# Freeing raw weight slabs by two counts, and rounding the next part's first block sums earlier, in a two-block transformer kernel

## The reference

```python
    x = layer_norm(ALPHA * x + mix, ln1_g, ln1_b)
    up = causal_dwconv(jnp.einsum('bsd,df->bsf', x, w_up), ffn_conv_w)
    a, b = jnp.split(up, 2, axis=-1)
    ffn = jnp.einsum('bsf,fd->bsd', jax.nn.silu(a) * b, w_down)
    return layer_norm(ALPHA * x + ffn, ln2_g, ln2_b)
```

## Time and profile before

| | |
|---|---|
| median of the runs | 2868.78 us |
| the profiled execution's own time | 2869.09 us |
| its span | 2867.3 us |
| PE busy | 2828.6 us, 15082 matmuls |
| ACT busy | 1717.4 us |
| DVE busy | 1488.8 us |
| POOL busy | 407.3 us |
| granted TensorE clock | 0.999 |
| HBM read | 482.23 MB, 169 GB/s over the span |

### The profile page before, as it was taken

One profiled execution on the slowest core, in us unless ns is written; L12 is line 12 of the kernel. 1 busy time (PEld: TensorE's weight loads), 2 busy tenths in 40 slices (PEclk: granted clock), 3 DMA queues, 4 the chain that ended last, 5 costly groups with the idle time before them and its releaser, 6 DMA issues.

```text
span 2867.3 us, 40191 instructions
## 1 busy us (share of the span) xinstructions
PE 2828.6 (99%) x15082; PEld 2422.0 (84%) x15082; DVE 1488.8 (52%) x2661; ACT 1717.4 (60%) x2505; POOL 407.3 (14%) x472
## 2 busy tenths in 40 slices
PE   9999999999999999999999999999999999999999
PEld 7989889889997778888987887898877788789887
DVE  6654636364444654644326115677654611656865
ACT  7676767566665765655556545656554744665564
POOL 1111111111111001111110111111111011111110
PEclk9999999999999999999999999999999999999999
DMA  9776767788887428888894797887879388778784
GB/s 246 159 155 139 176 135 160 159 191 193 190 191 164 88 53 190 196 195 191 193 192 101 169 195 164 193 189 170 198 165 200 82 188 194 168 184 183 181 195 118
DMA packets 137026, 486.82 MB, mean 170 GB/s; under 512 B 15344, under 2 KB 15600, under 8 KB 136720
## 3 DMA queue, kind: packets, MB, share of 16 engines
q0 software_dynamic: 67296, 233.01, 44.4%
q1 hardware_dynamic: 68688, 249.59, 30.9%
q10 hardware_dynamic: 864, 1.78, 0.2%
HBM read 482.23 MB, written 2.10 MB: 169 GB/s over the span
## 4 chain that ended last, share of the span: by engine, by line
PE 84%; DVE 7%; ACT 5%; DVEq 2%; issue 1%; DMA 0%; ACTq 0%
PE ps L1346 56%; PE ps L1515 10%; PE ps L1365 5%; PE ps L1774 3%; DVE arena L2716 1%; ACT arena_r L772 1%; DVE arena_r L2259 1%; PE ps L1465 1%; PE ps L1715 1%; PE ps L1694 1%; ACT wl L534 1%; ACT wh L527 1%; PE ps L1953 1%; ACT arena L1217 1%; DVEq L2248 1%
## 5 line engine op out<-in xcount | busy, mean ns | idle before, releaser
L527 ACT ACTIVATE wh<-raw 128x1024 fp32r<-128x1024 f32 (+2 forms) x465 | 468.4, 1007 | 671.1 <-PE ps L1346 579.5
L510 POOL DMA_DIRECT2D wl<-weights x465 | 405.4, 872 | 2424.6 <-ACT wl L534 2424.6
L1346 PE MATMUL ps<-HH,wh 128*128 128x512 f32 x1456 | 571.5, 393 | 2.9 <-DVE HL L2637 2.1
L1346 PE MATMUL ps<-HH,wl 128*128 128x512 f32 x1456 | 567.0, 389 | 0.0
L1346 PE MATMUL ps<-HL,wh 128*128 128x512 f32 x1456 | 566.8, 389 | 0.0
L534 ACT ACTIVATE wl<-raw 128x1024 fp32r<-128x1024 f32 (+2 forms) x465 | 463.8, 997 | 88.9 <-DVE arena L2255 88.9
L1346 PE MATMUL ps<-MH,wh 128*128 128x512 f32 x928 | 362.4, 391 | 1.0 <-DVE ML L2520 0.7
L1346 PE MATMUL ps<-MH,wl 128*128 128x512 f32 x928 | 361.2, 389 | 0.0
L1346 PE MATMUL ps<-ML,wh 128*128 128x512 f32 x928 | 361.1, 389 | 0.0
L1346 PEld LDWEIGHTS ps<-HH,wh 128*128 128x128 f32 x1456 | 273.4, 188 | 63.5 <-issue 3.8
L1346 PEld LDWEIGHTS ps<-HL,wh 128*128 128x128 f32 x1456 | 273.4, 188 | 57.4 <-issue 1.4
(11 more groups left out here) (395 smaller groups left out, 5036.0 us busy)
## 6 DMA issues: line engine op xcount, KB each, us to landing
raw<-weights SPq DMA_DIRECT2D x468, 512.0 KB, 5.2
wl<-weights POOLq DMA_DIRECT2D x369, 512.0 KB, 7.7
wl<-weights POOLq DMA_DIRECT2D x96, 384.0 KB, 6.8
XT<-x SPq DMA_DIRECT2D x4, 512.0 KB, 8.5
out<-XT SPq DMA_DIRECT2D x3, 512.0 KB, 2.7
arena<-tables POOLq DMA_DIRECT2D x1, 1024.0 KB, 10.5
arena<-table_h ACTq DMA_DIRECT2D x1, 640.0 KB, 6.3
arena<-swaps_a POOLq DMA_DIRECT2D x1, 576.0 KB, 8.2
```

What stands on the lines that cost most here:

```text
L510: pool.dma_start(wl[:, n, first:], weights[slab][:, first:], accum_op=ALU.add).then_inc(w_lo[n], 16)
L527: act_f(wh[:, n, at:w], raw[:, n, at:w], ACT.Copy)
L1346: op = mm(bank(g, t), w[:, slot, at:at + P], x[:, first + kt, :], start=(kt == 0 and w is wh and x is xh), stop=(kt == n_k - 1 and w is wl ...
```

## The change

SP waits for two counts before it reloads a slot: `w_hi` (ACT has written the low part) and the new `raw_taken` (DVE has read the raw slabs up to that slab). `raw_taken` counts in slabs: DVE raises it at its start to the first twisted slab's number, and after each `twist_raw` to the first slab of the next twisted set. `less_high_part` no longer waits for DVE. `twist_high` waits for `raw_taken` where it waited for `tw_raw`. The `twist_high` of the next part's first set moves from `down_before_twist` into the last iteration of `up_twisted`, ahead of the wait for `up_a` and the Silu. DVE's `twist_low` of that set is written at the end of `up_twisted`, which is the same place in DVE's order as before.

```diff
+        def raw_before(k):
+
+            firsts = sorted(TWISTED)[::2]
+            return firsts[k] if k < len(firsts) else n_slabs
...
                     sp.wait_ge(w_hi, i * SLOTS + (n + 1 - SLOTS))
+                    sp.wait_ge(raw_taken, i * SLOTS + (n + 1 - SLOTS))
                     sp.dma_start(raw[:, n, :], weights[i * SLOTS + n]).then_inc(w_load[n], 16)
...
             def less_high_part(s, w=SLAB):
                 n = s.mod(SLOTS)
                 at = 256 if twisted(s) else 0
-                if at:
-                    act.wait_ge(tw_raw, twist_of(s) + 1)
                 act_f(wl[:, n, at:w], raw[:, n, at:w], ACT.Identity, scale=-1.0).then_inc(w_hi, 1)
...
             def twist_high(k):
-                act.wait_ge(tw_raw, k + 1)
+                act.wait_ge(raw_taken, raw_before(k + 1))
                 act_f(t_hi[k % 2], t_raw, ACT.Copy).then_inc(tw_hi, 1)
...
-            def up_twisted(first, sets):
+            def up_twisted(first, sets, more):
...
-                    more = i + 1 < 2 * sets
-                    if more:
+                    last = i + 1 == 2 * sets
+                    if not last:
                         high_parts(s + (6 + 2 * i), 1)
+                    elif more:
+                        twist_high(k + 2 * sets)
                     act.wait_ge(up_a, k + i - 23)
                     act_f(up_silu, up_y[:, 0, :], ACT.Silu).then_inc(up_gate, 1)
...
             def down_before_twist():
...
                 high_parts(n + 4, 2)
-                twist_high(k)
                 c.take("group")
...
-                v.tensor_tensor(t_raw[:, 3], b21, t_raw[:, 2], ALU.subtract).then_inc(tw_raw, 1)
+                v.tensor_tensor(t_raw[:, 3], b21, t_raw[:, 2], ALU.subtract)\
+                    .then_inc(raw_taken, raw_before(k + 1) - raw_before(k))
...
             v.memset(warm, 1.0).then_inc(warm_ready, 1)
+            dve.sem_inc(raw_taken, raw_before(0))
```

More of the change, by code:

```diff
@@ L371, in block_program @@
         xs_ready, xs_sum, xs_hi, xs_done = sem("xs_ready"), sem("xs_sum"), sem("xs_hi"), sem("xs_done")
-        tw_raw, tw_hi, tw_low, tw_sum = sem("tw_raw"), sem("tw_hi"), sem("tw_low"), sem("tw_sum")
+        raw_taken, tw_hi, tw_low, tw_sum = sem("raw_taken"), sem("tw_hi"), sem("tw_low"), sem("tw_sum")
         tw_first, tw_copied = sem("tw_first"), sem("tw_copied")
@@ L438, in twisted @@
             return not s.terms and s.n in TWISTED
-        def twist_of(s):
-            at = [n for n in sorted(TWISTED) if n <= s.n]
-            return (len(at) - 1) // 2
+        def raw_before(k):
+            firsts = sorted(TWISTED)[::2]
+            return firsts[k] if k < len(firsts) else n_slabs
         def q_scale(j):
@@ L490, in _ @@
                 sp.wait_ge(w_hi, n + 1 - SLOTS)
+                sp.wait_ge(raw_taken, n + 1 - SLOTS)
                 sp.dma_start(raw[:, n % SLOTS, :], weights[n]).then_inc(w_load[n % SLOTS], 16)
@@ L1128, in up_part @@
                 if n_twist:
-                    up_twisted(first, n_twist)
+                    up_twisted(first, n_twist, first + sets in H_TWIST)
                 if paired(first):
@@ L2725, in up_twisted @@
                 low_part(2 * sets - 1)
+                if more:
+                    twist_low(k + 2 * sets)
             def down_before_twist(sets, scale):
@@ L2743, in up_part @@
                     k, g, s = c.at["tw"].n, c.take("group", 2), c.take("slab", 4)
-                    if more:
-                        twist_low(k)
                     residual_of(g, s + 2, 0)
```

## The result

The changed kernel takes 2853.44 us (median of six runs, 2851.98 to 2855.8), the kernel before 2868.99 us (six runs beside them, 2867.18 to 2870.71). The ratio is 0.9947, with a 95% interval of 0.9936 to 0.9958. That is a gain of 15.5 us, between 12.0 and 18.4 by the interval. The forecast was a gain of 12.2 us, to 2856.6.

A forecast was written before the change was run, and what follows sets the result against it. PE was taken as the bound, losing 14.63 us in the second block's twisted parts; less 1.6 us at boundaries and 0.8 us in down projections, the 12.2 us gain gave 2856.6 us, range 2853.8 to 2864.4.

The forecast's parts named there:

- The bound and its method: PE in the second block's twisted parts: matmul start times show 14.63 us lost, idle columns only 7.3 us.
- The block of the low parts: ACT's 6.19 us stand before a6's low part goes, `wl` transfers leave sooner, DVE's chain shortens by 1.35 to 1.43 us.
- The moved rounding: `twist_high` ahead of the last Silu: removes DVE's 4.05 us boundary wait, Silu 0.3 us later but covered, 0.7 to spare.
- What is next in line: Slab b0 lands at 1945.7 against PE's 1945.9; 1.6 us kept back for boundaries, 0.8 us for down projections.
- The sum: Whole execution: 14.63 - 1.6 - 0.8 = 12.2 us gained, to a median of 2856.6 us.
- The six stretches: Second block, two layers: parts A and B and C's twisted sets, start to start; PE loses 14.63 us there in sum.
- The range: Execution time from 2853.8 us, all 14.6 us gained and a little more, to 2864.4 us, the case of moved stalls.
- stalls would move to the boundary: Waits removed inside A or B return before B or C; only 4.6 us stays gained, 2864.2 us; chance 0.14.
- Slower transfers: Low transfers right behind raw loads share the way and land later, up to 8.7 us; 2861.3 us; chance 0.15.
- The moved rounding in the way: At four boundaries, late raw sums delay `twist_high`, the last Silu and PE's third down slab; 2876 us; chance 0.04.
- A change that does little: Some other unseen wait holds PE's starts where they are; within 3 us of before; chance 0.05.
- SP's added wait: One more register wait per slab on SP, taken as 0.05 us and hidden; 23 us if none were hidden.

## Why the prediction was off by 3 us

**The bound and its method: right.** By starts PE lost 14.6 us in the region, by idle columns 7.3; 13.5 came back there. The Trainium skill's warning about matmul busy share (Perfetto Trace Analysis, Identifying the Most-Contended Engine) agrees with this. The reason it gives does not: by the page pipelined matmuls look smaller in the trace, while here one of 512 columns shows 0.39 us and costs 0.2268 from start to start.

**The block of the low parts: right, and too small.** All waits for `wl` in the middle of a part went, and the low part at once behind the high one. The chain of DVE and ACT was forecast to become 1.35 to 1.43 us shorter and became 1.9 us shorter. From A's start to the first set's product on DVE it is 1.5 us, close to the forecast (1908.12 - 1884.63 = 23.49 before, and 1904.95 - 1882.97 = 21.98 after):

```profile
1904.95 0.69 DVE L2728 TENSOR_TENSOR arena<-arena 128x512 f32<-128x512 f32 x1
```

The other 0.4 us are a later gap in DVE's chain that I hadn't counted, this one in the kernel before:

```profile
1918.70 0.69 DVE L2724 TENSOR_TENSOR arena<-arena 128x512 f32<-128x512 f32 x1 [0.45 <-issue]
```

**The moved rounding: covered, as told, and needless.** That it cost nothing was right (the kernel with it behind the Silu), and so was the size of its cover (0.7 told, 0.6 found). But the prediction let this edit remove the waits at the four boundaries. Either edit removes them: with the move alone no wait for the additions is left, and with the counts alone none is left either. The step "Before, it stood behind b1, and DVE waited 4.05 us for it at the boundary" named a real cause in the kernel before, but did not ask whether it would still be one after the counts. It is not: the whole chain comes 1.9 us sooner, and that is enough, by 0.2 us.

**What is next in line: this is the step that failed.** "I take 0.4 us at each of the four boundaries, 1.6 us", and 0.8 us in the down projections: 2.4 us kept back in all. Measured were 0.3, 0.7 and 1.2 us in three profiles, mean 0.71. The place was right, since the waits that are left are for the transfer of the next part's first slab in both cases that exceed 0.5 us. But they come at two of the twelve boundaries of these profiles, not at each, and the down projections lost 0.1 us at most. POOL issues b0 53.25 us after A's start (1936.22 - 1882.97), 0.5 us sooner than the 53.77 that I had (1938.4 - 1884.63), so that it has 8.0 us to land where I left it 7.5 (7.6 at the last boundary of layer 2, where the issue comes 53.6 us after B's start), and it landed in 6.2 to 8.0 us, with 8.8 once. As the landings scatter up to and over that margin, how many come late is a matter of the execution.

**The sum.** Three terms together make the miss. The reserve, 2.4 - 0.7 = 1.7 us. The six stretches lose 14.18 us on average and not the 14.63 of the one profile: -0.45. The stretches outside, 1.6 us, for which the sum had no term: the prediction looked for the change's effect only where twisted parts meet. So 12.2 + 1.7 - 0.45 + 1.6 = 15.1 us, against 15.5 measured; with the 0.6 us ahead of the first twisted matmul and behind the last C it is 15.7, the difference of the profiled spans. Of the 1.6 us, the 0.5 in the stretch between the first block's MLPs lie in a spread of 341.0 to 343.5 us over all kernels tried and may be chance. Of the other 1.1 us, a small part is a wait for `wl` just ahead of part A, 0.2 us in each profile of the kernel before and in none of the changed one. The rest is scattered over many small gaps. Its cause is not settled, nor that the change gives it.

**The range.** Its low end took in "all 14.6 us, a little more for waits ahead of part A". This was 0.4 us for everything unseen, where 1.6 were wanted. The fault is that of a range drawn from a sum over one region. Its high end is printed as 2864.4, where the rival that sets it has 2864.2; that changes nothing.

**The rivals.** That stalls would move to the boundary: no, the excess of A and B, 1.7 to 3.9 us before, is at most 0.96 us in any of three profiles after. Slower transfers: no, see the landings; and the spread of 7.3 to 8.7 us by which the prediction had them disturb one another does not show that by itself. The moved rounding in the way: no; even doubled it costs 4 to 5 us and not 7. Its price of 2876 was also reckoned too high, as it kept nothing of the 4.6 us that the two parts C would still give back. A change that does little: no. SP's added wait: nothing, by four of them. No kernel tried beats the changed one by more than the noise; the one with the counts alone equals it with a smaller edit.

## What to carry to other kernels

When one count stands for two readers of a buffer, look at who must wait only so that the count stays true: here ACT did so for 88.9 us, and a count for each reader cost nothing and gave the whole 15 us. Read what a change can give from start to start of the work, not from idle columns, and measure the stretches outside the edited region as well, in several profiles of either kernel, before the range is drawn. And two edits that cure the same wait do not add up: 13.8 and 7.7 us apart, 13.5 together. A long wait beside the critical engine (4.05 us on DVE) cost time in one kernel and nothing in the next; what counts is the time in hand at the step that PE needs.

## What the runs showed of the hardware

The time to land of equal 384 KB transfers is spread widely within one execution (5.6 to 8.4 us for the eight around part A in the changed kernel's first profile) and changes between executions for the same slab: b0 of layer 2 took 6.2, 6.5 and 8.8 us in three profiles of the changed kernel. One such landing decides whether a boundary is late, by 0.5 to 1 us in the two cases here.

The granted clock of PE fell for a few us in some executions and not in others of the same kernel, at different places. The windows of the first profile of before and of its second (us, busy time and instructions of PE, PE's weight loads, DVE, ACT, POOL, then granted clock, DMA share, GB/s):

```profile
950.50:954.00 3.50, 3.46 (x19) 2.53 (x19) 1.48 (x3) 1.90 (x6) 0.28 (x1) 0.78 0.85 193
```

```profile
950.50:954.00 3.50, 3.50 (x24) 2.89 (x25) 1.38 (x4) 1.72 (x6) 0.10 (x1) 1.00 0.86 191
```

and of the changed kernel's first and second, 4 us sooner:

```profile
946.50:950.50 4.00, 4.00 (x11) 2.50 (x12) 2.31 (x8) 3.63 (x7) 0.72 (x1) 0.57 0.00 0
```

```profile
946.50:950.50 4.00, 3.63 (x19) 2.68 (x19) 3.65 (x12) 3.74 (x8) 0.57 (x1) 1.00 0.00 0
```

PE stood for 1.62 us just ahead of 946.5 in all four. In one the clock fell right behind that, in one 4 us later, behind another gap of 0.46 us, and in two not at all. At the lower level (1.2 GHz of 2.4) matmuls of 512 columns start 0.42 to 0.46 us apart and not 0.23. This accounts for a part of the spread of the stretch between the first block's MLPs, but not for all of it: the counts-only kernel took 342.94 us there with the clock at 1.00 throughout. So a difference of 1 to 2 us there between two single profiles says nothing of an edit.
